# Attention stage: two PSUM banks for the projection products alone, two for the rest, and the short products moved ahead of a block's projection

## What is computed

```python
scores = jnp.einsum("bqhrd,bshrd->bhrqs", qi, k) * scale
scores = scores - slopes[None, :, None, None, None] * dist
probs = jax.nn.softmax(scores, axis=-1)
w = probs[:, :, 0] - lam * probs[:, :, 1]
o = jnp.einsum("bhqs,bshe->bqhe", w, v)          # 128 queries at a time
o = rms_norm(o, subln_g) * (1.0 - lam_init)
y_attn = o.reshape(b, s, D_ATTN) * jax.nn.silu(g)
```

## Time and profile before

| what | us |
|---|---|
| median of 3 runs | 4297.82 (4294.3 to 4299.98) |
| the profiled execution | 4292.97 |
| its span | 4291.2 |
| PE busy in the span | 3805.8 (89%) |
| DVE busy, ACT busy | 2177.4 (51%), 1657.9 (39%) |

### The profile page before, as it was taken

One profiled execution on the slowest core, in us unless ns is written; L12 is line 12 of the kernel. 1 busy time (PEld: TensorE's weight loads), 2 busy tenths in 40 slices (PEclk: granted clock), 3 DMA queues, 4 the chain that ended last, 5 costly groups with the idle time before them and its releaser, 6 DMA issues.

```text
span 4291.2 us, 48849 instructions
## 1 busy us (share of the span) xinstructions
PE 3805.8 (89%) x20470; PEld 3153.1 (73%) x20470; DVE 2177.4 (51%) x2835; ACT 1657.9 (39%) x2243; POOL 528.4 (12%) x437
## 2 busy tenths in 40 slices
PE   6989999999988999888888886999888898879998
PEld 5768978788766777666666664988777777768988
DVE  3444243443464657444444453357777877753222
ACT  4323122211134556455555553133444544441122
POOL 0000010001011535000000000012222221210002
PEclk9989999999998999899999997999999999999999
DMA  2002011111111010100000004121111111143101
GB/s 87 30 25 79 30 64 50 49 48 41 49 51 50 30 40 11 46 26 21 24 25 25 25 30 154 40 75 44 38 33 38 45 35 50 33 153 139 40 30 64
DMA packets 196398, 211.31 MB, mean 49 GB/s; under 512 B 7943, under 2 KB 171732, under 8 KB 196180
## 3 DMA queue, kind: packets, MB, share of 16 engines
q1 hardware_dynamic: 190420, 187.22, 13.7%
q10 hardware_dynamic: 5760, 20.97, 1.3%
HBM read 174.62 MB, written 33.55 MB: 49 GB/s over the span
## 4 chain that ended last, share of the span: by engine, by line
PE 67%; DVE 15%; ACT 11%; issue 5%; DMA 1%; POOL 0%; SPq 0%; ACTq 0%; DVEq 0%; POOLq 0%
PE pd L211 58%; PE pq L211 6%; ACT t L311 2%; DVE t L2454 2%; DVE t L2755 1%; ACT t L2383 1%; PE pq L354 1%; DVE t L320 1%; PE pd L354 1%; DVE t L3158 1%; DVE t L2747 1%; DVE t L2472 1%; ACT t L2417 1%; DVE t L1788 1%; DVE t L3143 0%
## 5 line engine op out<-in xcount | busy, mean ns | idle before, releaser
L211 PE MATMUL pd<-t 128*128 128x512 f32 (+2 forms) x15920 | 3156.4, 359 | 215.6 <-DVE t L2279 40.6
L211 PEld LDWEIGHTS pd<-t 128*128 128x128 f32 x15920 | 2604.9, 194 | 713.4 <-issue 199.4
L211 PE MATMUL pq<-t 128*128 128x128 f32 (+5 forms) x3222 | 551.0, 333 | 106.5 <-ACT t L2799 19.3
L211 PEld LDWEIGHTS pq<-t 128*128 128x128 f32 (+2 forms) x3222 | 390.6, 182 | 215.0 <-issue 49.8
L311 ACT ACTIVATE t<-t 128x2048 fp32r<-128x2048 f32 (+2 forms) x150 | 245.4, 1637 | 760.9 <-PE pd L211 670.5
L320 DVE TENSOR_TENSOR t<-t 128x2048 fp32r<-128x2048 f32 (+2 forms) x150 | 297.9, 1987 | 318.7 <-ACT t L311 318.2
L1388 DVE TENSOR_TENSOR t<-pd,t 128x512 f32<-128x512 f32 x256 | 171.6, 688 | 122.9 <-PE pd L211 122.9
L2496 DVE COPY t<-pd 128x512 f32<-128x512 f32 x64 | 44.1, 690 | 288.4 <-PE pd L354 288.4
L354 PE MATMUL pd<-t 128*128 128x128 f32 x800 | 115.5, 294 | 70.9 <-DVE t L557 19.2
L1379 DVE TENSOR_TENSOR t<-t 128x512 fp32r<-128x512 f32 x64 | 45.9, 719 | 261.0 <-POOL t L1367 261.0
L2755 DVE SCALAR_TENSOR_TENSOR t<-t 128x1024 f32<-128x1024 f32 x120 | 177.4, 1478 | 0.3
(11 more groups left out here) (290 smaller groups left out, 2824.5 us busy)
## 6 DMA issues: line engine op xcount, KB each, us to landing
t<-in_w_in_dram SPq DMA_DIRECT2D x97, 512.0 KB, 4.1
t<-in_w_mlp_dram SPq DMA_DIRECT2D x32, 1024.0 KB, 5.3
t<-in_w_out_dram SPq DMA_DIRECT2D x20, 1024.0 KB, 5.1
t<-in_w_in_dram SPq DMA_DIRECT2D x16, 1024.0 KB, 5.3
t<-ym_scratch ACTq DMA_DIRECT2D x24, 512.0 KB, 7.3
t<-in_x_dram SPq DMA_DIRECT2D x16, 512.0 KB, 7.6
x_scratch<-t SPq DMA_DIRECT2D x16, 512.0 KB, 3.1
ym_scratch<-t SPq DMA_DIRECT2D x16, 512.0 KB, 2.6
```

The costliest lines, as they stand in the source:

```text
L211: ins = e.matmul(out, l, r, start=(first and j == 0), stop=(last and j == n - 1), skip_group_check=True)
```

## The change

Banks 0 and 1 of PD go to the projection alone, by the parity of the block. Everything else in the loop takes banks 2 and 3 in turn (`turns`), in the order of the calls. `at_bank` is `take` for a given bank: it waits until the last user of that bank has been read. On TensorE the values product, the transposes of values and the sum of squares now stand between the scores of block n + 2 and the projection of block n; on ScalarE their readers now stand between the exponentials of block n + 2 and the copy of wT. The wait of both copies for the values product is gone; ScalarE waits for it in `act_att_values`, which now comes first, and VectorE's copy follows TensorE's order.

```diff
+    def at_bank(e, i, *key):
+        PD.put(i, key)
+        e.vacant(PD, *key)
+        return PD.of(*key)
+
+    def fm(e, u, m0, th, v, *key, hold=False, bank=None):
+        b = e.take(PD, *key, hold=hold) if bank is None else at_bank(e, bank, *key)
...
-    def pe_att_ms(e, h, th):
+    def pe_att_ms(e, h, th, bank):
         if h >= 0:
-            b = e.take(PD, "oms", h, th)
+            b = at_bank(e, bank, "oms", h, th)
...
+        turns = cycle((2, 3))
         for n in range(BLOCKS):
             h, tt = divmod(n, NT)
             if n + 2 < BLOCKS:
                 pe_att_scores(e, n + 2)
+            if tt % 4 == 0 and n:
+                pe_att_values(e, n - 4, next(turns))
+            if tt >= 6 and h < 7:
+                pe_att_vt(e, h + 1, tt - 6, next(turns))
+            if owed(n)[0] >= 0:
+                pe_att_ms(e, *owed(n), next(turns))
             if h < 7:
                 if tt % 2 == 0:
                     pe_att_unit(e, h + 1, KIND[tt])
-                pe_att_fm(e, h + 1, KIND[tt], tt % 2)
-                if tt >= 6:
-                    pe_att_vt(e, h + 1, tt - 6)
-            pe_att_ms(e, *owed(n))
-            if tt % 4 == 0 and n:
-                pe_att_values(e, n - 4)
+                pe_att_fm(e, h + 1, KIND[tt], tt % 2, n % 2)
             for q2 in range(2):
-                b = e.take(PD, "wT", n, q2)
+                b = at_bank(e, next(turns), "wT", n, q2)
...
                 scores(n + 2)
+            if tt % 4 == 0 and n:
+                act_att_values(e, n - 4)
+            if tt >= 6 and h < 7:
+                act_att_vt(e, h + 1, tt - 6)
+            act_att_ms(e, *owed(n))
             e.wait_ge(*at["wT", n, 0])
-            if tt % 4 == 0 and n:
-                e.wait_ge(*at["AV", h if tt else h - 1, 0 if tt else 1])
             e.copy(WT[:, 0:4, tile(tt % 4)], four(PD.of("wT", n, 0)[:, :])).then_inc(
                 *at.inc("act", "wTc", n, 0, free=("wT", n, 0)))
-            if tt % 4 == 0 and n:
-                act_att_values(e, n - 4)
-            act_att_ms(e, *owed(n))
             if h < 7:
                 act_att_out(e, h + 1, KIND[tt], tt % 2)
-                if tt >= 6:
-                    act_att_vt(e, h + 1, tt - 6)
```

More of the change, by code:

```diff
@@ L2 @@
 from contextlib import ExitStack
-from itertools import chain, islice
+from itertools import chain, cycle, islice
 import numpy as np
@@ L330, in sp_unit @@
                     e.i.dma_start(dst, src).then_inc(*at.landed(f"wr{i % 3}", "w_landed", i))
-    def fm(e, u, m0, th, v, *key, hold=False):
-        b = e.take(PD, *key, hold=hold)
+    def at_bank(e, i, *key):
[4 more added lines that the diff above has]
+        b = e.take(PD, *key, hold=hold) if bank is None else at_bank(e, bank, *key)
         for k in range(8):
@@ L2209, in pe_att_unit, with pe_att_fm, pe_att_vt @@
         open_unit.append(pe_unit(e, W2in, [(FROM[kind] + h * 128, 128)]))
-    def pe_att_fm(e, h, kind, th):
-        fm(e, open_unit[-1], 0, th, 2, "a" + kind, h, th)
+    def pe_att_fm(e, h, kind, th, bank=None):
+        fm(e, open_unit[-1], 0, th, 2, "a" + kind, h, th, bank=bank)
         if th == 1:
             pe_done(open_unit[-1])
-    def pe_att_vt(e, h, th):
-        b = e.take(PD, "avT", h, th)
+    def pe_att_vt(e, h, th, bank=None):
+        b = e.take(PD, "avT", h, th) if bank is None else at_bank(e, bank, "avT", h, th)
         e.wait_ge(*at["avc", h, th])
@@ L2307, in owed, with pe_att_values @@
         return {2: (h - 1, 1), 5: (h, 0)}.get(tt, (-1, 0))
-    def pe_att_ms(e, h, th):
+    def pe_att_ms(e, h, th, bank):
         if h >= 0:
-            b = e.take(PD, "oms", h, th)
+            b = at_bank(e, bank, "oms", h, th)
             e.wait_ge(*at["osq", h, th])
             mms(e, b[:, :], [(ones[:, :], tmp.of("osq", h, th)[:, :])]).then_inc(*at.inc("pe", "oms", h, th))
-    def pe_att_values(e, n):
+    def pe_att_values(e, n, bank):
         h, th = n // 8, n // 4 % 2
-        b = e.take(PD, "AV", h, th)
+        b = at_bank(e, bank, "AV", h, th)
         for m in range(n, n + 4):
@@ L2355, in pe_stage_att @@
             at.also("pe", ("s", n))
-        pe_att_values(e, 60)
-        pe_att_ms(e, 7, 1)
+        pe_att_values(e, 60, next(turns))
+        pe_att_ms(e, 7, 1, next(turns))
     def act_att_ms(e, h, th):
```

## The result

The changed kernel takes 4262.4 us (median of 4 runs, 4258.0 to 4264.9) against 4298.6 before: ratio 0.9916 (95% interval 0.9899 to 0.9934), 36 us less. The profiled execution took 4258.0 with a span of 4256.2, 35.0 less than that of before. The forecast was 26 less.

A forecast was written before the change was run, and what follows sets the result against it. The softmax loop through VectorE and ScalarE, not TensorE, sets the pace in k and q blocks. Gains 27.5 (five heads) + 1.65 + 5.3, less 2.5 and 5.4, taken as 26: 4297.8 to 4272 us, range 4255 to 4294.

The forecast's parts named there:

- The reading of the profile: Attention stage: TensorE waits 115.3 us for ring banks, but in k and q blocks the softmax loop sets the pace.
- D1 to D3: From VectorE's diff in tt 1 to that in tt 3: stays at 25.9 us, the loop covering a new wait.
- eight pieces: One head cut at diffs (D) and ends of wT transposes (P): 101.3 us at full clock, 109.33 before.
- The wait of tt 5: Second wT bank held by the sum of squares until the logarithm: a 2.4 us pause of TensorE.
- D5 to P5: From diff in tt 5 to the end of its wT transposes: 5.35 us becomes 9.05, loss 3.7.
- the clock term: Slow TensorE work behind new pauses: 1.7 to 4.3 us a head, taken as 2.55.
- the pause of tt 7: Second wT bank held by value transposes until read: 4 us pause behind the projection, then 1.7 us of slow clock.
- Head 6 with the last head: End of the attention stage: gain 5.3 up to diff of tt 7, then losses of 2.5 and 5.4 us.
- (a): Rival: slow clock after the pauses of tt 2, 5 and 7 outweighs the gain; 22 us slower, 4320, chance 0.08.
- (b): Rival: gain given back in full by clock terms or a longer loop; within 8 us, 4295, chance 0.15.
- (c): Rival: shared banks never bind because ScalarE runs far enough ahead; 4207 us, chance 0.05.
- (d): Rival: all 115 us of waits and the clock are gained; 4143 us, chance 0.02.

The follow-up runs named there:

- only ScalarE's readings move: Changed kernel with ScalarE's readings of k and q ahead of the copy of wT in tt 0 to 2: 4260.5 us, ratio 0.9914.
- both pauses filled: Changed kernel plus products nobody reads, 14 in tt 7 and 8 in tt 5 of each of the first seven heads: 4249.5 us, ratio 0.9889.
- one fill: Changed kernel plus 14 products nobody reads in tt 7 of each of the first seven heads: 4256.0 us, ratio 0.9902.
- the banks alone: Banks of the changed kernel with the order of the kernel before on TensorE and ScalarE: 4309.7 us, ratio 1.0031 against the kernel before.
- the sum moved: Changed kernel with the sum of squares in the projection bank that is idle in its block: 4278.2 us, ratio 0.9958.
- the transposes moved: Changed kernel with the value transposes behind the projection again, in the projection bank idle in their block: 4250.0 us, ratio 0.9893.

## Why the prediction was right, and where it was off

**The reading of the profile** held. Removing 115 us of waits gave 36, because the loop through VectorE and ScalarE sets D1 to D3 whatever the banks do (25.66 to 25.93 in the kernel before, in each half and in the changed kernel, and 0.9 less when only ScalarE's readings move), and because two of the removed waits came back at the second wT bank. Of eight pieces six lie within 0.25 us of their terms without a clock term. The wait of tt 5, bounded by a row of the last head, came out at 2.74 us. The sum for D5 to P5, 9.05, had taken the table load at the 1.28 us of the earlier trace rows; 9.16 was measured. By the Trainium skill, "ScalarE: Activation LUTs", "What ACT_TABLE_LOAD costs", a drain of about 1.4 us beside each load would have made it about 10.4 (an estimate from that page's figure); the trace does not agree.

**Off in size: the clock term.** I took 2.55 us a head: 1.7 behind the pause of tt 7 and half of 1.7 behind that of tt 5. With both pauses filled the head takes 100.66, so the clock costs the changed kernel 1.6 us, all of it at tt 7; behind tt 5 its clock is 1.00 and D5 to D7 23.6 us in all five steady heads. In the first head it did fall there, and that head came to 99.70, near the 99.95 forecast. The difference to the forecast, 1.6 a head, is thus 0.95 of clock and 0.65 of the pieces, and over five heads 8 of the 10 us that were missed between 26 and 36. Two pauses alike had different outcomes in the earlier trace rows; taking half was fair as a mean. In the changed kernel all five steady heads came out alike, so the half fitted neither outcome, and both should have been cases of their own. Had the clock fallen at tt 5 in each of them, as it does with one fill (1.4 us a head), the gain would have been near 29 us by estimate: closer to the forecast by luck, with the mechanism no better foreseen.

**Off in a small term: the end.** Head 6 with the last head was to cost 2.6 and cost 3.5.

**Rivals.** (a) The slow clock never came near the 8 us a head at which it would decide: 1.6. The kernel with the banks alone is the nearest thing to it: each long pause costs clock there, but its steady heads are no slower than before, and its 13 us lie at the two ends of the stage. What the Trainium skill, "TensorE: Matmul & The Clock Gate", "A second HAM failure mode: psum-queue depth-cycling", describes, short idle times that swing the clock, is in all three traces: 0.91 before, 0.92 with the banks alone, 0.97 in the changed kernel. It doesn't say which of them is the fastest. (b) was not the case. (c) and (d) are out by the pauses themselves. I had weighed the change as one; that its two halves pull in opposite directions, - 60 and + 13 alone, could have been drawn from the pieces, since all new waits came from the shared banks, and I did not draw it.

**Left open.** Why the clock falls behind the pause of tt 5 in the runs with the sum moved, with the transposes moved (from the fourth head on), with one fill and with the readings moved, and not in the steady heads of the changed kernel, though the pause is 2.7 to 2.9 us in all: the runs show that it does, with one fill and with the readings moved in each of the five steady heads, and not why.

## What to carry to other kernels

A wait is priced by what stands behind it, not by its length: ask of each bank who reads it last and how late that reader stands in its own list, and give a short product a bank whose next user comes late (here the idle projection bank, with both short products: 4262 to 4226 us). Split a change into its halves when one of them adds sharing; here the half that named the change, the private banks, cost 26 us of what the other gave. Where pauses of some 2 to 5 us remain on TensorE, as in these runs, a gain of 1 to 2 us a head may be lost to the clock (readings moved) or come from it alone (both pauses filled), so judge an edit by the pieces of the trace and not by the total alone.

## What I had not expected

Useless products made the kernel faster: 154 of them by 13 us. And moving work on ScalarE in tt 0 to 2 went with a slower clock of TensorE from diff of tt 5 to that of tt 7, three blocks later and in code untouched by the edit: 1.00 to 0.93, 1.4 us in each of the five steady heads.
